# The last four expert blocks of a mixture-of-experts kernel: residual rows and blocks added in PSUM, with an order of their own

## The reference, cut to what matters

```python
def expert_block(args):
    xb, e = args
    hdn = jax.nn.silu(xb @ w_gate[e]) * (xb @ w_up[e])
    return hdn @ w_down[e]
...
out = zeros.at[slot_tok].add(ys * slot_gate[:, None])
...
h = h + hier_moe(rmsnorm(h, ffn_norm), ...)
return rmsnorm(h, final_norm)[:, N_META:]
```

## Time and profile before

| what | value |
|---|---|
| median of 3 runs | 2472.19 us (2471.54 to 2479.42) |
| the profiled execution's own time | 2473.32 us |
| its span, first to last instruction | 2471.3 us |
| granted TensorE clock, mean over the span | 0.955 |
| TensorE, VectorE, ScalarE busy | 88%, 39%, 20% |
| DMA rate while the expert weights are loaded | about 428 GB/s |

### The profile page before, as it was taken

The page is one execution under the profiler, slowest core; times in us unless marked ns, Lnnn a source line. Parts: engine busy times, 40 slices in busy tenths (PEclk is TensorE's granted clock), DMA queues, the critical chain, the costliest instruction groups (busy, mean ns, idle before and its releaser), DMA issues.

```text
span 2471.3 us, 34403 instructions
## 1 busy us (share of the span) xinstructions
PE 2185.4 (88%) x14459; PEld 1530.6 (62%) x14459; DVE 971.9 (39%) x1715; ACT 499.1 (20%) x1029; POOL 0.2 (0%) x4
## 2 busy tenths in 40 slices
PE   8999999999999999999999997777777777777776
PEld 5888888766564888888654655444444444444443
DVE  3777653154443444453313525323222222222223
ACT  3111100244323111100221311111111111111112
POOL 0000000000000000000000000000000000000000
PEclk8999999999999999999999998988988898998988
DMA  7565721411202224221401033999999999999997
GB/s 276 170 227 182 247 94 47 102 30 48 94 1 68 69 85 133 68 94 47 146 14 69 1 158 125 421 428 428 428 429 428 428 429 429 429 429 429 429 429 300
DMA packets 149364, 549.04 MB, mean 222 GB/s; under 512 B 8320, under 2 KB 101776, under 8 KB 123552
## 3 DMA queue, kind: packets, MB, share of 16 engines
q1 hardware_dynamic: 149280, 547.82, 56.3%
HBM read 545.70 MB, written 2.10 MB: 222 GB/s over the span
## 4 chain that ended last, share of the span: by engine, by line
PE 62%; DMA 31%; DVE 4%; ACT 1%; issue 1%; SPq 1%; ACTq 0%; PEldq 0%; DVEq 0%; PEld 0%
DMA slots<-in_expert_w_up 29%; PE ps L824 18%; PE ps L867 11%; PE ps L1358 7%; PE ps L914 4%; PE ps L1005 2%; PE ps L1084 2%; PE ps L1279 2%; PE ps L920 2%; DMA slots<-in_w_mod 2%; PE ps L938 1%; PE ps L1079 1%; PE ps L1082 1%; PE ps L1224 1%; PE ps L947 1%
## 5 line engine op out<-in xcount | busy, mean ns | idle before, releaser
L1358 PE MATMUL ps<-slots,xT 128*32 128x256 f32 x4052 | 296.4, 455 | 195.8 <-DMA slots<-in_expert_w_up 175.7
L1358 PEld LDWEIGHTS ps<-slots,xT 128*32 128x32 f32 x4052 | 155.0, 130 | 324.3 <-DMA slots<-in_expert_w_up 183.9
L824 PE MATMUL ps<-hT,slots 128*128 128x256 f32 x1408 | 314.1, 382 | 3.7 <-ACT hT L1478 3.4
L824 PEld LDWEIGHTS ps<-hT,slots 128*128 128x128 f32 x1408 | 268.4, 191 | 42.8 <-issue 3.8
L824 PE MATMUL ps<-slots 128*128 128x256 f32 x1056 | 238.0, 382 | 5.5 <-DVE slots L1882 5.5
L824 PEld LDWEIGHTS ps<-slots 128*128 128x128 f32 x1056 | 201.1, 191 | 33.5 <-issue 6.3
L2392 DVE COPY hT<-ps 128x128 f32<-128x128 f32 x64 | 18.5, 289 | 419.1 <-PE ps L1365 419.1
L2398 DVE TENSOR_TENSOR big<-ps,big 128x512 f32<-128x512 f32 x128 | 88.3, 691 | 222.9 <-PE ps L1391 222.9
L1376 PE MATMUL ps<-slots,hT 128*32 128x256 f32 x2048 | 123.8, 381 | 30.6 <-DVE hT L2392 30.6
L1752 ACT ACTIVATE xT<-ps 32x256 f32<-32x256 f32 x256 | 95.9, 374 | 261.6 <-PE ps L1376 259.4
L1746 ACT ACTIVATE big<-ps 32x256 f32<-32x256 f32 x128 | 47.8, 373 | 400.9 <-PE ps L1358 400.2
(11 more groups left out here) (364 smaller groups left out, 2596.3 us busy)
## 6 DMA issues: line engine op xcount, KB each, us to landing
slots<-in_expert_w_down SPq DMA_DIRECT2D x64, 2048.0 KB, 25.0
slots<-in_expert_w_gate SPq DMA_DIRECT2D x63, 2048.0 KB, 18.5
slots<-in_expert_w_up SPq DMA_DIRECT2D x63, 2048.0 KB, 23.0
slots<-in_w_mod SPq DMA_DIRECT2D x18, 2048.0 KB, 12.0
slots<-in_w_gate SPq DMA_DIRECT2D x22, 1024.0 KB, 5.5
slots<-in_w_up SPq DMA_DIRECT2D x22, 1024.0 KB, 8.1
slots<-in_w_down SPq DMA_DIRECT2D x8, 2816.0 KB, 10.5
slots<-in_w_in SPq DMA_DIRECT2D x24, 512.0 KB, 5.8
```

The source lines that it names most:

```text
L824: last = mm(bank[:, g], lhs[:, g, k], rhs[:, k], start=(first and g == 0 and k == 0), stop=(k == 3), skip_group_check=True)
L1358: last = mm(ps[at:at + CAP, j, 0:256], xsT[:, k, i * CAP:(i + 1) * CAP], w[g][k][:, 256 * h:256 * (h + 1)], start=(k == 0), stop=(k == KC ...
```

## The change

The last quad gets code of its own on TensorE and ScalarE. The eight PSUM banks become the sums of the four token tiles (`final_banks[t]` is banks 2t and 2t+1).

- `mixed(t, g)` puts the residual rows into the bank by a product with the identity; `first_blocks(t, g)` adds blocks 0 and 1 (64 rows of gates and outputs). Both are issued ahead of `gate_up(3)`, but for tile 3, whose banks 6 and 7 still serve blocks 2 and 3.
- The gates of blocks 2 and 3 are turned by 16 products each with the identity, which place a block's 32 gate rows four times, in the four groups of 32 partitions. So the output of `down`, which stands in four such groups, is copied whole (one copy of 128x256 in place of four of 32x256, `last_rows`), and `last_block(i, t, c)` adds it by products of 32 rows, one per group c and tile t. They are issued in two rounds of six for tiles 0 to 2 and four rounds of two for tile 3, with a drain of TensorE behind each round.
- `turn_hidden(1)`, `down(1)` and `rows_out(1)` come after the gate turning and five residual products; `turn_hidden(2)` comes ahead of `gate_up(3)`, no longer behind it.
- ScalarE does one square root of a constant behind the copy of block 2's rows, and waits for `s_ha` (hidden rows of block 3) ahead of that copy.
- VectorE's last eight adds are gone; square and final product read PSUM.

The arguments `end` of `gate_up`, `turn_hidden`, `down`, `gate_sigmoid`, `hidden` and `hidden_in` only choose the bank. The rest of the diff:

```diff
+        last_rows = [mo[:, 3072 + 256 * k:3328 + 256 * k] for k in range(2)]
+        last_gates = [part(10240 + 512 * k, 512).rearrange("p (t m) -> p t m", t=NT) for k in range(2)]
+        final_banks = [ps[:, 2 * t:2 * t + 2, :] for t in range(NT)]
+
+        def gate_up_bank(i, end):
+            return 4 + i if end and i >= 2 else i % 2
+
+        def turned_hidden(i, end):
+            bank, at = (4 + i, 256) if end and i >= 2 else (6 + i % 2, 0)
+            return ps[:, bank, at:at + 4 * CAP]
+
+        def down_bank(i, end):
+            return 4 + i if end and i >= 2 else 2 + i % 2
...
+            def last_quad(q):
+
+                def mixed(t, g):
+                    mm(final_banks[t][:, g, :], ident, h2[:, t, g * 512:(g + 1) * 512], start=True, stop=False, skip_group_check=True)
+
+                def first_blocks(t, g):
+                    mm(final_banks[t][:, g, :], gate_rows[0:2 * CAP, t, :], ys[0:2 * CAP, g * 512:(g + 1) * 512], start=False, stop=False,
+                       skip_group_check=True)
+
+                def last_block(i, t, c):
+                    rows = slice(CAP * c, CAP * (c + 1))
+                    return mm(final_banks[t][:, c // 2, c % 2 * 256:(c % 2 + 1) * 256], last_gates[i - 2][rows, t, :], last_rows[i - 2][rows, :],
+                              start=False, stop=(i == 3), skip_group_check=True, tile_position=(CAP * c, 0))
+                gate_up(1, q)
+                combine(before(q))
+                turn_hidden(0)
+                down(0, q)
+                gate_up(2, q, end=True)
+                pe.wait_ge(s_sum, value(q, 8, 0))
+                turn_gates(q)
+                for i in (2, 3):
+                    for t in range(NT):
+                        for c in range(4):
+                            last = mm(ps[c * CAP:(c + 1) * CAP, (5, 0)[i - 2], t * P:(t + 1) * P], gate_hot[:, t, i * CAP:(i + 1) * CAP], ident,
+                                      start=True, stop=True)
+                    last.then_inc(s_gt, 1)
+                mixed(0, 1)
+                pe.wait_ge(s_yc, value(q, 4, 1))
+                mixed(1, 0)
+                pe.wait_ge(s_gtc, value(q, 1, 1))
+                mixed(2, 0)
+                pe.wait_ge(s_gtc, value(q, 1, 3))
+                mixed(2, 1)
+                mixed(0, 0)
                 turn_hidden(1)
-                down(3, q)
+                down(1, q)
+                pe.wait_ge(s_yc, value(q, 4, 2))
+                mixed(1, 1)
+                for t in range(3):
+                    for g in range(2):
+                        if t == 2 and g == 1:
+                            pe.wait_ge(s_ha, value(q, 4, 3))
+                        first_blocks(t, g)
+                turn_hidden(2, True)
+                gate_up(3, q, end=True)
+                down(2, q, True)
+                pe.wait_ge(s_ha, value(q, 4, 4))
+                mm(turned_hidden(3, True), ident, ident, start=True, stop=True)
+                turn_hidden(3, True)
+                pe.wait_ge(s_yc, value(q, 4, 3))
+                for odd in range(2):
+                    for t in range(3):
+                        for c in ((t + odd) % 2, (t + odd) % 2 + 2):
+                            last_block(2, t, c)
+                    pe.drain()
+                mixed(3, 0)
+                down(3, q, True)
+                first_blocks(3, 0)
+                pe.wait_ge(s_yc, value(q, 4, 4))
+                mixed(3, 1)
+                for odd in range(2):
+                    for t in range(3):
+                        for c in ((t + odd) % 2, (t + odd) % 2 + 2):
+                            last = last_block(3, t, c)
+                            if odd:
+                                last.then_inc(s_cmb, 1)
+                    pe.drain()
+                first_blocks(3, 1)
+                for i in (2, 3):
+                    for odd in range(2):
+                        for c in (odd, odd + 2):
+                            last = last_block(i, 3, c)
+                            if i == 3 and odd:
+                                last.then_inc(s_cmb, 1)
+                        pe.drain()
...
                 quad((i, 1))
-            quad((n_more, 1), end=True)
-            combine((n_more, 1))
+            last_quad((n_more, 1))
 
...
+            def last_quad(q):
+                gate_sigmoid(1, q)
+                rows_out(0, q)
+                gate_sigmoid(2, q, True)
+                gates_in(q)
+                for i in (2, 3):
+                    act.wait_ge(s_gt, value(q, 1, i))
+                    av(last_gates[i - 2].rearrange("p t m -> p (t m)"), ps[:, (5, 0)[i - 2], :], ACT.Copy).then_inc(s_gtc, 1)
+                rows_out(1, q)
+                gate_sigmoid(3, q, True)
+                act.wait_ge(s_ha, value(q, 4, 4))
+                for i in (2, 3):
+                    act.wait_ge(s_my, value(q, 4, i + 3))
+                    av(last_rows[i - 2], ps[:, down_bank(i, True), 0:256], ACT.Copy).then_inc(s_yc, 1)
+                    if i == 2:
+                        av(fox_s[:, 15:16], eps_col[:, 0:1], ACT.Sqrt)
...
             for t in range(NT):
 
-                act.wait_ge(s_sum, value((n_more, 1), 8, 2 * t + 2))
-                av(sq_row, h2[:, t, :], ACT.Square, accum_out=glst[:, 32 + t:33 + t]).then_inc(s_fsq, 1)
+                act.wait_ge(s_cmb, value((n_more, 1), 8, 6 if t < 3 else 8))
+                av(mo[:, 0:D].rearrange("p (b n) -> p b n", b=2), final_banks[t], ACT.Square, accum_out=glst[:, 32 + t:33 + t])\
+                    .then_inc(s_fsq, 1)
                 act.wait_ge(s_fsq, t + 1)
                 av(glst[:, 36 + t:37 + t], glst[:, 32 + t:33 + t], ACT.Sqrt, scale=1.0 / D, bias=eps_col[:, 0:1]).then_inc(s_fst, 1)
...
-                v.scalar_tensor_tensor(out=h2[:, t, :], in0=h2[:, t, :], scalar=glst[:, 40 + t:41 + t], in1=gain_row,
-                                       op0=ALU.mult, op1=ALU.mult).then_inc(s_fin, 1)
+                v.scalar_tensor_tensor(out=h2[:, t, :].rearrange("p (b n) -> p b n", b=2), in0=final_banks[t], scalar=glst[:, 40 + t:41 + t],
+                                       in1=gain_row.rearrange("p (b n) -> p b n", b=2), op0=ALU.mult, op1=ALU.mult).then_inc(s_fin, 1)
             for t in range(NT):
-                add_rows((n_more, 1), t)
-                if t >= 1:
-                    final_row(t - 1)
-            final_row(NT - 1)
+                final_row(t)
```

More of the change, by code:

```diff
@@ L1361, in gate_up, with turn_hidden, down @@
                             last.then_inc((s_mg, s_mu)[g], 1)
-            def turn_hidden(j):
+            def turn_hidden(i, end=False):
+                dst, j = turned_hidden(i, end), i % 2
                 for c in range(4):
-                    last = nc.tensor.transpose(ps[:, 6 + j, c * CAP:(c + 1) * CAP], hrow[j].rearrange("p (m c) -> p c m", c=4)[:, c, :],
+                    last = nc.tensor.transpose(dst[:, c * CAP:(c + 1) * CAP], hrow[j].rearrange("p (m c) -> p c m", c=4)[:, c, :],
                                                ident[0:CAP, 0:CAP])
                 last.then_inc(s_ta, 1)
-            def down(i, q):
+            def down(i, q, end=False):
                 j = i % 2
+                bank = down_bank(i, end)
                 pe.wait_ge(filled[3 * j + 2], value(q, 32, first[3 * j + 2] + 16 + 16 * (i // 2)))
@@ L1392, in combine, with quad @@
                        stop=True).then_inc(s_cmb, 1)
-            def quad(q, start=False, end=False):
+            def quad(q, start=False):
                 gate_up(1, q)
@@ L1406, in quad @@
                 gate_up(3, q)
-                turn_hidden(0)
+                turn_hidden(2)
                 down(2, q)
                 pe.wait_ge(s_gtc, value(q, 1, 1))
[L1410 to L1416, removed]
-                turn_hidden(1)
@@ L1418, in quad @@
-                down(3, q)
+                pe.wait_ge(s_oh, value(q, 1, 1))
+                pick_rows(quad_hot)
+                gate_up(0, behind(q))
+                turn_hidden(3)
+                down(3, q)
+            def last_quad(q):
[29 more added lines that the diff above has]
+                mixed(0, 0)
+                turn_hidden(1)
+                down(1, q)
[38 more added lines that the diff above has]
+                        pe.drain()
@@ L1745, in gate_sigmoid @@
                 for h in range(2):
-                    last = av(sg[j][:, 256 * h:256 * (h + 1)], ps[CAP * h:CAP * (h + 1), j, 0:256], ACT.Sigmoid)
+                    last = av(sg[j][:, 256 * h:256 * (h + 1)], ps[CAP * h:CAP * (h + 1), gate_up_bank(i, end), 0:256], ACT.Sigmoid)
                 last.then_inc(s_eg, 1)
@@ L1753, in rows_out, with quad @@
                 last.then_inc(s_yc, 1)
-            def quad(q, end=False):
+            def quad(q):
                 for i in range(QUAD):
@@ L1758, in quad @@
                         gate_sigmoid(i + 1, q)
-                    elif not end:
+                    else:
```

(14 more changed lines are left out.)

22 lines of the change are left out of this document (12 added, 10 removed).

## The result

The changed kernel is slower. Its median is 2484.19 us (2476.77 to 2488.17, 17 runs) against 2473.28 us of the kernel before beside it (2471.05 to 2483.30, 17 runs); their ratio is 1.003, 95% interval 1.0018 to 1.0042, so the loss is clear of noise. The forecast was 2469.2 us. The runs of each kernel spread over some 12 us, and the size of the loss depends on what is compared: the medians are 10.9 us apart, the means (2482.74 and 2475.74) 7.0, the lowest runs 5.7.

The account below looks back on a forecast made before the run. The expert stage was taken as bound by late weights, 29% of the span on up-weight loads. Terms -0.1 + 2.0 - 1.35 - 3.5 = -2.95, taken as -3.0 from 2472.19, gave 2469.2 us; range 2465.8 to 2474.0.

Parts of the forecast that it names:

- Part 1: Up to the end of block 3's gate and up: added work offsets the full clock's gain of 2.2, -0.1 us.
- price of a product: TensorE work ahead of block 3's gate and up: 0.433 us per 512-column product, from 64 taking 27.70.
- Part 2: From block 3's gate and up to the start of its down: two rounds and a residual product added, +2.0 us.
- The rounds: Block 2's two rounds of six 32-row products ahead of block 3's down: 1.15 us each with drain, 2.3 together.
- serial row groups: Rival for the 32-row products: groups run one after the other, 1.8 us a round, +2.6, 2471.8; chance 0.13.
- open loads: Rival for the 32-row products: loads not hidden either, 2.5 us a round, +5.4, 2474.6; chance 0.08.
- Part 3: From block 3's down to the first square: one copy for four, then products and two rounds, 3.0 us, -1.35.
- Part 4: From the first square to the end: VectorE's adds go and the table load moves, 10.6 us for 14.1, -3.5.
- The table load: ScalarE's 1.28 us load, forecast free behind block 2's row copy; rival: it returns before the first root, 2470.5, chance 0.04.
- The clock: Rival: clock stays low for block 3's gate and up, up to +3.6 us, 2472.8; chance 0.08.
- Shape changes: Rival: each change of tile shape on TensorE costs a drain, five on the path, +1.3 us, 2470.5; chance 0.09.
- The last down weights: Block 3's down: weights issued later, at about 2437.7, still land at 2450.4; at worst 2454.6, 1.7 us more.

Follow-up runs that it names:

- second profile: Changed kernel run again with no edit, clock at 1.00 until the last rows: 53.1 us from the last quad's first transposes to the end (before 47.5).
- better order: Changed kernel with block 1's down first and the six first-block products behind block 3's gate and up: 49.4 us, last quad's first transposes to end (before 47.5).
- experiment on the kernel before: Kernel before plus only the early square root of a constant: 45.2 us, last quad's first transposes to end (before 47.5); first square to end 13.1 against 14.1.

## Why the prediction was wrong

**Part 1 failed, at its price of a product.** I took 27.70 us for 64 products of 512 columns as 0.433 for each product that the code writes. The 64 are two each: 32 written products. The hint stood in the earlier trace rows: gate and up of one block is x64, and the code writes 8 x 2 x 2 = 32. So five residual products cost 4.5, not 2.2; the last residual product and six first-block products 6.4, not 3.0; the small gate products, priced by the same reading of a count, 2.1, not 1.5 (1.9 to 2.4 in the three profiles). These three terms are 6.3 too low. By the second profile the part ends 6.5 later than before, where I had -0.1. The Trainium skill, FP8 and Floating Point Precision, TensorE Precision Notes, gives a true fp32 product four passes through the array; an estimate from that page, 512 columns x 4 at 2.4 GHz, is 0.85 for a written product, and the two rows of 0.433 agree. The experiment without the first-block products shows the doubled price on the path, and the one with the better order shows that not all of the work can be hidden. Gate and up starts 8.7 us later than before, and the full clock gives 2.2 of that back. The full clock itself came as forecast, 3.66.

**Part 2** was right in sign and 0.6 short by the second profile: +2.6 for +2.0. The residual product was 1.05 rather than 0.43, mostly by the same error. The rounds cost 2.3, as forecast, by the experiment without them, though each has twelve traced products, not six: my pace was taken from L1120, whose x8 are four written products, and four row groups overlap more than its two. Two errors cancelled there, and the right figure is luck. The rivals of serial row groups and of open loads are out.

**Part 3** gave +0.1 for -1.35: behind block 3's down come one first-block and one residual product, 1.05 each, where I had 0.38 (the copy, with the first-block product beside it) and 0.43, and the rounds take 2.4 for 2.05.

**Part 4 held**: 10.6 and 10.3 for 10.6, VectorE's products 1.39 to 1.8 apart. Tile 3's products on TensorE end 4.2 to 4.5 behind the first square, for 3.9, and so hold up ScalarE's fourth square by up to 0.5. The table load is 1.0 of the gain, by the experiment on the kernel before; that the rest goes with VectorE's adds is what is left over, and no run shows it by itself.

**The clock** was a rival in the wrong place. Gate and up ran at 1.00 each time; the fall came later, in block 2's rounds and block 3's down, in one of three profiles of the changed kernel, where it costs 3.2, and for a shorter time in one of its variants. Where it falls, it adds to the loss of 5.6.

**Shape changes** do cost something; that rival was right in kind and too dear. In the version without row groups a residual product stands between products of its own shape, and from its start to the next it takes 2466.43 - 2465.57 = 0.86. In the second profile, between products of other shapes, it takes 2462.82 - 2461.77 = 1.05. That is 0.19 more, and for the three written products of 512 columns behind block 3's transposes some 0.6 of the loss. I had read L1120's start as no gap, but products of one shape start 0.16 ahead of the modelled end before them (the tail in part 1), and L1120 only 0.07: 0.09 was lost there too. The better order shows the same: its products of 64 rows end at 2460.55 + 4.55 = 2465.10, and those of 32 rows begin at 2465.03.

The last down weights were in time in every version with row groups. In the first profile they were issued at about 2446.1 and landed 9.9 later, for 16.9 before: the later issue did not delay their landing by much, as I had taken it.

As measured in the second profile, the four parts are 6.5 + 2.6 + 0.1 - 3.6 = +5.6, without a fall of the clock, where the forecast had -3.0. The range ended at 2474.0, since the rivals doubted the row groups, the clock and the table load, and none of them doubted the price of a product.

## What to carry to other kernels

Before a row's duration is used as a price, its count is to be set against the number of instructions that the code writes for that row; here x64 for 32 written products was enough to see that each is two. Work put ahead of a late transfer is free up to the transfer's landing and on the path from there, so the fill is added up against the wait, and what doesn't fit is left where it overlaps something else. A change that spares VectorE and ScalarE by giving TensorE more products pays on the path for each product that doesn't fit into a wait: with all of them the stretch is 1.9 us longer than before even in the better order, and in the version without row groups, with six residual products ahead of gate and up, it is 4.5 shorter.

## What the runs showed that I had not expected

The granted clock fell to its lower level, 1.2 GHz, in stretches in which TensorE is shown busy for over 0.9 of the time: in the first profile of the changed kernel from 2463.5 to 2470.3, behind gate and up at the full level, 0.97 of standing still, and some 2 us of 32-row products. The same instructions in two further executions ran at 2.4 GHz throughout. Whether it is the thin products, the drains or the stand ahead of them that leaves the clock open to fall was not settled: the runs that took one of these away didn't fall, but neither did two of the three profiles of the changed kernel itself.

Products of 32 rows in four row groups overlap well even with a load each: 2.36 us for 24 traced products of 256 columns in two rounds, where the same number with 128 rows took 5.45.
